# Pooled groups two and three: the output projection by seven block products, with one product of the second half moved ahead

## What is computed

```python
def pool_mixer(h, w_in, w_group, scale, w_out):
    u, z = jnp.split(h @ w_in, 2, axis=-1)          # 2048 channels each
    p = causal_multiscale_pool(u).reshape(B, S, N_POOL_GROUPS, GROUP_WIDTH)
    y = jnp.einsum('bsgc,gcd->bsgd', p, w_group).reshape(B, S, A_WIDTH_2) * scale
    return (y * jax.nn.silu(z)) @ w_out
```

## Time and profile before

| | us |
|---|---|
| median of 3 runs | 2352.72 (2350.76 to 2353.45) |
| the profiled execution | 2353.32 |
| its span, first to last instruction | 2351.4 |
| TensorE busy | 2324.9 |
| VectorE / GpSimd / ScalarE busy | 1537.1 / 1255.9 / 859.8 |
| output part of group 2, 192 matmuls | 1758.7 to 1802.2 |

### The profile page before, as it was taken

How to read it: one execution, slowest core, us unless ns; L and a number is a source line. 1 busy time by engine, 2 the same in 40 slices (tenths; PEclk the granted TensorE clock), 3 DMA queues, 4 the chain that set the end, 5 groups by cost and what they waited for, 6 DMA issues and landing times.

```text
span 2351.4 us, 32286 instructions
## 1 busy us (share of the span) xinstructions
PE 2324.9 (99%) x11585; PEld 1943.6 (83%) x11585; DVE 1537.1 (65%) x1839; ACT 859.8 (37%) x1596; POOL 1255.9 (53%) x724
## 2 busy tenths in 40 slices
PE   9999999999999999999999999999999999999998
PEld 7888789888888888888888888788878788889887
DVE  7825555524578777877877777774672967147885
ACT  5212555512543222222222443122231244157773
POOL 4533954143135666676777424573754733467743
PEclk9999999999999999999999999999999999999999
DMA  6511001031011333333332211112121123210034
GB/s 220 157 45 50 19 19 37 1 117 54 10 42 50 117 125 125 117 124 125 117 123 63 63 45 45 59 57 73 54 81 62 58 67 110 79 37 25 22 112 139
DMA packets 67420, 179.08 MB, mean 76 GB/s; under 512 B 7010, under 2 KB 13924, under 8 KB 65200
## 3 DMA queue, kind: packets, MB, share of 16 engines
q1 hardware_dynamic: 57840, 148.03, 19.3%
q10 hardware_dynamic: 9104, 27.51, 3.5%
q0 software_dynamic: 368, 2.10, 0.5%
HBM read 161.84 MB, written 15.77 MB: 76 GB/s over the span
## 4 chain that ended last, share of the span: by engine, by line
PE 76%; DVE 6%; issue 4%; POOL 2%; ACT 1%; DMA 0%; POOLq 0%; DVEq 0%; ACTq 0%; SPq 0%
PE ps L705 21%; PE ps L706 21%; PE ps L708 21%; PE ps L855 4%; PE ps L833 3%; PE ps L843 2%; DVE trail L3538 1%; PE ps L2410 1%; POOL split_lo L1658 1%; PE ps L2426 1%; ACT p L956 1%; PE ps L2395 1%; PE ps L2396 1%; PE ps L2425 1%; PE ps L509 0%
## 5 line engine op out<-in xcount | busy, mean ns | idle before, releaser
L705 PE MATMUL ps<-h_hi,split_hi 128*128 128x512 f32 x1546 | 607.2, 393 | 3.4 <-DVE h_lo L3220 1.3
L706 PE MATMUL ps<-h_lo,split_hi 128*128 128x512 f32 x1546 | 601.9, 389 | 0.0
L708 PE MATMUL ps<-h_hi,split_lo 128*128 128x512 f32 x1546 | 536.5, 389 | 0.0
L1516 POOL TENSOR_TENSOR split_hi<-raw,cf 128x1024 fp32r<-128x1024 f32 x64 | 125.2, 1956 | 427.8 <-PE ps L708 373.2
L705 PEld LDWEIGHTS ps<-h_hi,split_hi 128*128 128x128 f32 x1546 | 290.9, 188 | 63.9 <-issue 2.2
L708 PEld LDWEIGHTS ps<-h_hi,split_lo 128*128 128x128 f32 x1546 | 290.9, 188 | 61.0
L706 PEld LDWEIGHTS ps<-h_lo,split_hi 128*128 128x128 f32 x1546 | 291.2, 188 | 56.3 <-issue 0.2
L1605 POOL TENSOR_TENSOR split_lo<-raw,split_hi 128x512 fp32r<-128x512 f32 x144 | 232.9, 1635 | 193.9 <-ACT split_hi L2723 193.4
L1658 POOL TENSOR_TENSOR split_lo<-raw,split_hi 128x512 fp32r<-128x512 f32 x84 | 128.1, 1534 | 179.2 <-ACT split_hi L2884 179.2
L2723 ACT CAST split_hi<-raw 128x512 fp32r<-128x512 f32 x144 | 86.7, 622 | 283.9 <-PE ps L708 204.0
L1518 POOL TENSOR_TENSOR split_lo<-raw,split_hi 128x1024 fp32r<-128x1024 f32 x64 | 178.4, 2787 | 5.0
(11 more groups left out here) (508 smaller groups left out, 5213.2 us busy)
## 6 DMA issues: line engine op xcount, KB each, us to landing
raw<-in_strips SPq DMA_DIRECT2D x208, 256.0 KB, 2.8
raw<-in_strips SPq DMA_DIRECT2D x86, 512.0 KB, 3.4
ada_raw<-in_ada SPq DMA_DIRECT2D x64, 512.0 KB, 3.7
memw_raw<-in_mem_strips SPq DMA_DIRECT2D x8, 512.0 KB, 6.1
xT<-in_xT ACTq DMA_DIRECT2D x4, 1024.0 KB, 8.1
x_spill_d<-xT ACTq DMA_DIRECT2D x1, 3584.0 KB, 10.1
xT<-x_spill_d ACTq DMA_DIRECT2D x2, 1792.0 KB, 9.9
out_T<-out_sb SPq DMA_DIRECT2D x13, 256.0 KB, 2.2
```

What stands on the lines that cost most here:

```text
L705: pe.matmul(acc[:, a:b], w_hi, hi[:, a:b], start=first, stop=False)
L706: pe.matmul(acc[:, a:b], w_hi, lo[:, a:b], start=False, stop=False)
L708: mm = pe.matmul(acc[:, a:b], w_lo, hi[:, a:b], start=False, stop=last)
L1516: pool.tensor_tensor(hi, raw[:, r, :], ones[:, 0:1].to_broadcast([P, D]), ALU.mult).then_inc(hi_split, 1)
```

## The change

In groups 1 and 2 the output projection is made in two halves of four output tiles (`quad` 0 and 1), each by seven block products over 2x2 blocks of weights (two output tiles by two input tiles) and 2x2 blocks of tokens. A product is 12 matmuls in two parts of 6. The order on TensorE is `OUT_ORDER`: products 0 and 1 of the first half, product 0 of the second, then 2 to 6 of the first and 1 to 6 of the second. Group 3 keeps its eight output tiles.

- Weights: GpSimd makes four sums of weight blocks for each half and seven low halves (`out_forms`); SyncE loads the halves in another order, and one of them twice.
- Tokens: products 1 and 5 use the difference of the two token halves, and 2, 4 and 6 sums of four blocks. VectorE, GpSimd (`neg_rest`) and ScalarE make them, with high and low halves. They are put into tokens 512 to 1023 of tiles 0 to 5 of `h_hi` and `h_lo` (`neg_place`; `h_plain` is the same place as plain float32). ScalarE saves these tokens to memory in group 1 (`h_keep_d`), brings them back after each of groups 1 and 2 (`h_fetch`) and rounds them (`h_round`); products 5 and 6 of the next group's first quad wait for that.
- Results: each product adds into two banks, some on top of an earlier product that VectorE has read (`OUT_AFTER`), and VectorE adds each of 28 halves to `xT` (`out_sum`).
- The group loops of TensorE and GpSimd are written out instead of looping. Waits and counts change accordingly, some semaphores are shared, and the strips of the output weights are laid out anew on the host.

The core of the diff (waits that only have new counts, and the layout, are left out):

```diff
+OUT_BANKS = (((4, 6), (5, 7), (2, 3)), ((0, 1), (5, 7), (2, 3)))
+OUT_ORDER = [(0, 0), (0, 1), (1, 0)] + [(0, i) for i in range(2, 7)] + [(1, i) for i in range(1, 7)]
+OUT_READS = ([0, 2, 1, 3, 4, 5, 6], list(range(7)))
+OUT_BANK = [0, 1, 0, 2, 0, 1, 0]
+OUT_AFTER = {2: 0, 4: 2, 5: 1, 6: 4}
+OUT_SECOND, OUT_LATE = (1, 4, 6), (1, 2, 4, 5)
+NEG_T = {2: 4, 3: 2, 4: 0}
...
+        def neg_place(g, m, low, tiles):
+
+            at = slice(NEG_T[m] + tiles.start, NEG_T[m] + tiles.stop)
+            return (h_lo if low else h_hi)[:, at, HALF:T]
...
+            def load_out(g, quad):
+                for i, d in ((2, 0), (3, 1), (4, 2), (6, 3)):
+                    group_split(sp, g, out_form(quad, i))
+                    load_group_half(g, 12 + 2 * quad + d // 2, d % 2)
...
             with sp.Fori(1, POOL_GROUPS - 1) as g:
                 load_group(g)
-                for d in range(4):
-                    group_split(sp, g, GROUP_OUT_AT + 4 + d)
-                    load_group_half(g, POOL_STRIPS + d // 2, d % 2)
-            load_group(POOL_GROUPS - 1)
+                group_split(sp, g, out_form(1, 0))
+                load_group_half(g, 10, 1)
+                for quad in range(2):
+                    load_out(g, quad)
...
-
-            with pool.Fori(1, POOL_GROUPS) as g:
+                pool.wait_ge(form_sum, 24 * g + (SUM_BASE + 4 * q + n))
+
+            def out_forms(g, quad):
+
+                j = 10 + 2 * quad
+
+                def out_low(i, of=quad):
+                    group_low(g, out_form(of, i), OUT_SOURCE[i] if (of, i) != (1, 0) else a12)
+
+                group_half(pool, g, j, 0)
+                if quad == 0:
+                    out_low(0)
+                group_half(pool, g, j + 1, 0)
+                group_half(pool, g, j + 1, 1)
+                pool.tensor_tensor(pool_form, a21, a22, ALU.add).then_inc(form_sum, 1)
+                out_low(1)
+                if quad == 0:
+                    early_half(pool, g)
+                    out_low(0, 1)
+                summed(g, 4 + quad, 1)
+                pool.tensor_tensor(a21, a21, a11, ALU.subtract).then_inc(form_sum, 1)
+                group_split(pool, g, out_form(quad, 1))
+                pool.tensor_tensor(pool_form, a11, pool_form, ALU.subtract).then_inc(form_sum, 1)
+                for kk in range(2 if quad == 0 else 0):
+                    if kk == 0:
+                        gate_high(pool, g, 3)
+                    neg_made(pool, g, 1 + kk)
+                    pool.tensor_tensor(neg_full(g, 3, kk), neg_full(g, 2, kk), neg_full(g, 3, kk), ALU.add).then_inc(neg_rest, 1)
+                    if kk:
+                        gate_made(pool, g, 5)
+                    pool.tensor_tensor(neg_full(g, 4, kk), neg_full(g, 2, kk), gates[:, 2 + kk, 0:HALF], ALU.add).then_inc(neg_rest, 1)
+                    if kk == 0:
+                        out_low(2)
+                if quad:
+                    out_low(2)
+                group_half(pool, g, j, 1)
+                group_split(pool, g, out_form(quad, 2))
+                pool.tensor_tensor(pool_form, a12, pool_form, ALU.add).then_inc(form_sum, 1)
+                for i in range(3, 7):
+                    out_low(i)
+
+            for g in range(1, POOL_GROUPS):
...
-                for d in range(12):
+                for d in range(4 if g < POOL_GROUPS - 1 else 12):
                     group_half(pool, g, 8 + d // 2, d % 2)
                     group_low(g, GROUP_TILE_AT + d, raw_half(d // 2 % 2, d % 2))
+                for quad in range(2 if g < POOL_GROUPS - 1 else 0):
+                    out_forms(g, quad)
...
+            def out_token(g, i, kk):
+
+                if i in (2, 4, 6):
+                    return neg_tile(g, (2, 3, 4)[i // 2 - 1], 0, kk), neg_tile(g, (2, 3, 4)[i // 2 - 1], 1, kk)
+                k, tok = kk + (2 if i in (3, 5) else 0), out_tokens[i in (1, 5)]
+                return gated_hi_tile(k)[:, tok], y_lo[:, k, tok]
+
+            def out_forms_of(g):
+
+                for quad, i in OUT_ORDER:
+                    p = out_form(quad, i)
+                    group_split(pe, g, p)
+                    if quad == 0:
+                        if i in (2, 4, 6):
+                            neg_lower(pe, g, i)
+                        else:
+                            gate_lower(pe, g, {0: 1, 1: 4, 3: 6, 5: 7}[i])
+                    for part in range(2):
+                        if (quad, i) == (0, 0):
+                            gate_made(pe, g, 1 + part)
+                        elif (quad, i) == (1, 0):
+                            gate_made(pe, g, 3)
+                        elif (quad, i) == (0, 3):
+                            gate_made(pe, g, 5)
+                        elif (quad, i) == (1, 1):
+                            out_summed(pe, g, 0, 5, part)
+                        elif (quad, i) == (1, 3):
+                            out_summed(pe, g, 0, 3, part)
+                        elif i in OUT_AFTER:
+                            out_summed(pe, g, quad, OUT_AFTER[i], part)
+                        slot, w = group_at(g, p)
+                        product(pe, bank(OUT_BANKS[quad][OUT_BANK[i]][part]), slot,
+                                [(w + 2 * part + kk, *out_token(g, i, kk)) for kk in range(2)], HALF, start=i in (0, 1, 3), skip=True)\
+                            .then_inc(form_done if part else pool_tile, 1)
...
+                    elif n == 5 and g > 1:
+                        pe.wait_ge(h_rounded, 6 * (g - 2) + 2)
                     elif n == 6:
                         sums_made(pe, 1, 12)
+                        if g > 1:
+                            pe.wait_ge(h_rounded, 6 * (g - 1))
...
+                            free=p_free if t == 3 and g < POOL_GROUPS - 1 else None).then_inc(form_done, 1)
+
+                if g < POOL_GROUPS - 1:
+                    out_forms_of(g)
+                    return
...
+            def neg_high_tile(g, m, kk):
+                if m == 2:
+                    neg_made(act, g, 1 + kk)
+                else:
+                    neg_rest_made(act, g, 2 * kk + m - 2)
+                act.copy(neg_tile(g, m, 0, kk), neg_full(g, m, kk)).then_inc(neg_hi, 1)
+
+            def h_fetch(m, done):
+                a = NEG_T[m]
+                for low in range(2):
+                    act.dma_start(h_plain[:, NK * low + a:NK * low + a + 2, HALF:T], h_keep_d[:, low, a:a + 2, :]).then_inc(done, 16)
+
+            def h_round(m):
+                for low, of in enumerate((h_hi, h_lo)):
+                    a = NEG_T[m]
+                    act.copy(of[:, a:a + 2, HALF:T], h_plain[:, NK * low + a:NK * low + a + 2, HALF:T]).then_inc(h_rounded, 1)
+
+            def out_high(g, n, t, tok):
+                gate_made(act, g, n)
+                act.copy(gated_hi_tile(t)[:, tok], gated_tile(t)[:, tok]).then_inc(pool_yhi, 1)
...
                         group_through(act, g, GROUP_TILE_AT + 3)
-                        gated_high_tile(g, 2)
-                        gated_high_tile(g, 3)
+                        if g == POOL_GROUPS - 1:
+                            out_high(g, 3, 2, slice(0, T))
+                            out_high(g, 4, 3, slice(0, T))
                         act.wait_ge(x_spilled, 16 * g)
                         act.dma_start(xT[:, 6:8, :], x_pair_d).then_inc(x_again[0], 16)
+                        if g < POOL_GROUPS - 1:
+                            neg_high_tile(g, 2, 1)
                     group_high(g + p // GROUP_FORMS, p % GROUP_FORMS)
...
-                    if p in (32, 33):
-                        gated_high_tile(g, p - 32)
-                    if g == POOL_GROUPS - 1 and p >= 36:
-                        key_square(p - 36)
+                    if p == GROUP_OUT_AT:
+                        out_high(g, 1, 0, slice(0, T))
+                    if p == GROUP_OUT_AT + 1:
+                        out_high(g, 2, 1, slice(0, T))
+                    if g < POOL_GROUPS - 1:
+                        if p == GROUP_OUT_AT + 1:
+                            if g == 1:
+                                act.wait_ge(h_kept, 64 + 96)
+                            act.copy(neg_whole(g, 3, slice(0, 2)), gates[:, 0:2, out_tokens[0]]).then_inc(pool_yhi, 1)
+                        if p == GROUP_OUT_AT + 2:
+                            neg_high_tile(g, 2, 0)
+                            out_place_free(act, g, 1)
+                            out_high(g, 3, 2, slice(0, T))
+                            neg_high_tile(g, 3, 0)
+                            neg_high_tile(g, 4, 0)
+                        if p == GROUP_OUT_AT + 3:
+                            neg_high_tile(g, 3, 1)
+                            out_high(g, 4, 3, out_tokens[1])
+                            out_high(g, 5, 3, out_tokens[0])
+                            neg_high_tile(g, 4, 1)
+                    if g == 1 and p in (8, 10, 12, 14, 16, 18):
+                        m, low = 2 + (p - 8) // 4, (p - 8) // 2 % 2
```

(104 more changed lines are left out.)

157 lines of the change are left out of this document (113 added, 44 removed).

## The result

The changed kernel takes 2356.60 us (median of 20 executions, 2354.41 to 2359.74); the kernel before took 2352.45 in the same comparison (20 executions, 2350.73 to 2354.81). The ratio is 1.0019, 95% interval 1.0013 to 1.0025: 4.2 us slower, between 3.1 and 5.9. The forecast was 2355.8 us for the median, "the same".

A forecast was written before the change was run, and what follows sets the result against it. TensorE, busy 99% of the span, was taken as the bound. Each of two groups gains 5.4 us and loses 7.0, +3.1 us in all: 2356.4 us for the profiled execution, 2355.8 for the median, own range 2351.8 to 2357.8.

The forecast's parts named there:

- What is removed: TensorE, output projection of groups 1 and 2: 168 matmuls for 192, at 0.2266 us each, saves 5.44 us a group.
- The lower of the two bounds: Extra cost of products 2, 4 and 6 reading `h_hi` and `h_lo`: bounds 0 and 0.5 us a group, 0 taken.
- Turns: VectorE and GpSimd operations that read two SBUF tensors alternate, overlapping by 0.14 us: 1.69 us for one of each.
- without turns, 2343.2: Faster rival: the engines take no turns, product 2 is 0.7 us late and nothing else; chance 0.16.
- Product 1: Output part: starts 4.2 us after product 0 instead of 2.72, 1.5 us late, waiting for VectorE's `difference_low(1)`.
- product 2: Output part: starts at 11.8 us instead of 8.16, 3.6 us late in all, because `neg_low(2, 1)` blocks VectorE's queue.
- Product 6: Output part: starts at 26.1 us where 19.0 would be in time, 7.1 us late, behind VectorE's residuals and subtractions.
- the sum: VectorE's work before product 6: 10.2 us plus 4.6 for five of seven subtractions meeting GpSimd, at 0.9 us each.
- The slower rival: VectorE never catches up: product 6 starts at 29, 9.7 us lost a group, 2361.2 us; decides past 26.9; chance 0.20.
- Nothing more in the second half: Output part behind product 6: second-half weights are ready in time for products 1 to 3, so no more is lost.
- The loss: Output parts of groups 1 and 2: 7.0 us lost against 5.4 gained, +1.6 us a group.
- Costed at nothing: Edits given no time: saving and bringing back tokens, ScalarE's roundings, SP's loads, unrolled loops, and the clock.

The follow-up runs named there:

- e4: Changed kernel with the second operand of VectorE's seven token subtractions behind `neg_low(2, 1)` read from a PSUM bank instead of SBUF: 2351.64 us, ratio 0.9996 to before.
- e3: Changed kernel with GpSimd's sums ahead of low halves and VectorE's residuals and token subtractions interleaved, same operations: 2344.31 us, ratio 0.9964 to before.
- e1: Changed kernel with product 0's two residuals and the third token tile's low half ahead of `neg_low(2, 1)` on VectorE: 2352.66 us, ratio 0.9999 to before.
- e5: Changed kernel without bringing back the saved tokens (twelve transfers and twelve ScalarE roundings left out): 2355.60 us, ratio 1.0015 to before.
- e8: Changed kernel; in group 2 ScalarE makes the third quad's first weight high half before a pooled high half: 2356.39 us, ratio 1.0017 to before.
- e7: e3 with the second half's first product back at the head of the second half: 2349.23 us, ratio 0.9987 to before.
- e6: Changed kernel with the second half's first product back at the head of the second half: 2352.80 us, ratio 1.0001 to before.
- e9: e3 with group 2's third-quad first weight high half made before a pooled high half on ScalarE: 2343.31 us, ratio 0.9963 to before.

## Why the prediction was right, point by point

- *What is removed.* 24 matmuls a group at 0.2267 us, also on `h_hi` and `h_lo`: where no wait stands between them, the changed kernel's products 1 to 6 of the second half take 2.72 us each. The lower of the two bounds was right; 5.44 us stands.
- *Turns.* 1.70 us start to start for 1.69. This was the step on which the sign hung: without turns, 2343.2. e4 shows them as a cause, and e3 comes to 2344.3 by order alone, since fewer operations meet.
- *Product 1* started at 4.28 (4.2), *product 2* at 11.75 (11.8). VectorE's idle time of "about 5 us" stands in two places: 3.86 us ahead of `neg_low(2, 1)`, and 1.0 of its own 1.68, since an operation that waits for its turn is shown as running. It ended at 10.94 (11.0). e1 shows that the blocked head was worth 2.7 us a group.
- *Product 6* started at 26.56 (26.1). The seven subtractions behind `neg_low(2, 1)` took 9.85 us in the changed kernel and 4.48 in e4 (3.37 + 2.38 + 1.57 + 2.53 against 3 x 1.27 + 0.67): 5.4 us of turns, for which the sum had 4.6. Five of the seven met an operation, as forecast, at 1.0 us each. The sum's 0.9 had no row behind it: the middle of its 0 to 1.15 is 0.58, and with that the turns are 2.9 us, product 6 starts at 24.4 and a group comes out even. So the sign of the forecast hung on a figure that was chosen and not read, and there it was lucky. The slower rival's start of 29 is a slip as well: 7 x 1.15 us in place of 4.6 gives 29.5. The point at which the slower rival would have decided, 26.9, was missed by 0.3 us.
- *Nothing more in the second half*: no wait behind product 6, right. Of the waits, 4.7 us a group are for VectorE, 0.9 for GpSimd and 0.4 for neither; "hardly for GpSimd" was a little too strong.
- *The loss* was 7.6 for 7.0 us a group, so +2.2 for +1.6. Five waits of the trace sum to 6.0 us. Each stop costs TensorE 0.24 us more than its bracket shows: the first matmul behind it starts 0.16 us later than bracket and pace give, and the next one follows at 0.31 us where 0.23 is the pace. A sixth stop, at product 4, has no bracket at all:

```profile
1780.22 0.39 PE L775 MATMUL ps<-p_hi,split_lo 128*128 128x512 f32 x1
1780.61 0.47 PE L772 MATMUL ps<-h_hi,split_hi 128*128 128x512 f32 x1
1780.92 0.40 PE L773 MATMUL ps<-h_lo,split_hi 128*128 128x512 f32 x1
```

Six stops make 1.4 us, which with the 6.0 is 7.5 of the 7.6; in e4, with two stops, 0.5 and 3.2 make its 3.7. No step of the prediction had that. The page shows this time as busy, and with the clock's 1.6 us it is most of the 4.3 us by which the busy time fell less than the missing matmuls.

- *Costed at nothing.* The reload: right within what can be measured (e5). The clock: right for the changed stretch (1.00 in both); outside it, it fell near 1709 us in the profiled execution, for 1.6 us, and not in that of the kernel before. The next group's quads: the prediction looked only for a wait on ScalarE there and found none, but GpSimd's chain in the third quad lost turns to VectorE, a wait of 1.5 to 1.8 us in all kernels here but e8 and the kernel before.
- *The total.* Two output parts give +4.4 us and the medians differ by 4.15. The forecast of +3.1 is short by the 0.6 us a group above. The profiled execution, 2359.23 for a forecast of 2356.4, has in addition the 2.1 us of group 2's quads and 0.5 of group 3's; against that its group 1 output part starts 0.9 us earlier (1613.60 for 1614.54), within the 1611.9 to 1615.0 at which it starts in the eleven profiled executions. The forecast drew its line for "the same" at 0.2%; the ratio, 1.0019 with an interval to 1.0025, lies so close to it that the side on which it fell is chance.

## What to carry to other kernels

Before work is taken from the bound engine and given to two others, lay their queues side by side and price each pair of operations by what it reads: here two SBUF inputs on VectorE beside GpSimd cost a whole turn (1.69 us for 0.68), and with one PSUM operand none (0.64). Then look at each queue's head: put nothing that waits for a late input ahead of something that could run, on every engine that the moved step touches. Here the change itself was good for 8 us, and the order of some ten instructions decided whether it was 4 us slower or 8 us faster.

## What the runs showed of the hardware that was not expected

- A lead of 0.03 us, in e7 of 0.01, was enough for VectorE to go first, and the lost turns add up along a chain: GpSimd's two low halves took 4.57 us together, 2.64 in e8. The Trainium skill's "SBUF — State Buffer", Who interferes with whom, says that the order of issue decides who blocks; the rows of the changed kernel and e8 agree.
- TensorE's granted clock fell to the 1.2 GHz level inside an otherwise busy stretch, at 0.57 on the mean of 4 us, after a wait of 1.77 us. It fell in the same way after waits of 1.84 us (e6, third quad: 0.60 on the mean of 4 us) and 1.96 (e7, second output part), and did not after 1.73 (e5, third quad), 1.77 (both output parts of the changed kernel) and 2.31 (e6, output part). And it fell between 1356 and 1363 us in seven of the eleven profiled executions (0.76 on the mean of 7 us) without a wait, and not in e1, e6, e8 and e9. Each fall cost some 1.6 us; what decides it stays open.
- A stop of TensorE costs 0.24 us beyond the idle time that its row shows, and a short one can show no idle time at all (0.39 us start to start for 0.23).
